# Two recurrent mixers with other engines for their gate products and another order in their last tiles; a gated mixer whose out-projection starts with other banks

## The reference

```python
def _rglru_mixer(h, w_in, conv_w, conv_b, gate_a_w, gate_a_b, gate_x_w, gate_x_b, lam, w_out):
    gate, xr = jnp.split(h @ w_in, 2, axis=-1)          # 1280 columns each
    gate = jax.nn.gelu(gate)
    xr = _causal_dwconv(xr, conv_w) + conv_b            # 4 taps
    xh = xr.reshape(b, s, A_HEADS, A_HEAD_DIM)
    r  = sigmoid(einsum(xh, gate_a_w) + gate_a_b)       # 16 heads of 80
    ig = sigmoid(einsum(xh, gate_x_w) + gate_x_b)
    log_a = -8.0 * r * softplus(-lam)
    a = exp(log_a)
    u = sqrt(-expm1(2.0 * log_a)) * (ig * xr)
    hs = scan over time of h[t] = a[t] * h[t-1] + u[t]
    return (hs * gate) @ w_out

def _sgu_mixer(h, w_in, norm_g, w_s, s_bias, w_out):
    u, v = split(gelu(h @ w_in))
    v = _rmsnorm(v, norm_g)
    mixed = (lower-triangular w_s applied over chunks of 128 tokens to v) + s_bias
    return (u * mixed) @ w_out
```

## Time and profile before

| | us |
|---|---|
| median of 3 runs | 2772.72 (2772.41 to 2773.76) |
| the profiled execution, its own time | 2773.85 |
| its span | 2772.0 |
| TensorE busy | 2708.9 (98%) |
| VectorE busy | 1778.0 (64%) |
| ScalarE busy | 1202.8 (43%) |
| GpSimd busy | 202.2 (7%) |
| mean granted TensorE clock | 0.992 of full |

### The profile page before, as it was taken

How to read it: one execution, slowest core, us unless ns; L and a number is a source line. 1 busy time by engine, 2 the same in 40 slices (tenths; PEclk the granted TensorE clock), 3 DMA queues, 4 the chain that set the end, 5 groups by cost and what they waited for, 6 DMA issues and landing times. The chain is left out here.

```text
span 2772.0 us, 46096 instructions
## 1 busy us (share of the span) xinstructions
PE 2708.9 (98%) x17940; PEld 2422.9 (87%) x17940; DVE 1778.0 (64%) x2341; ACT 1202.8 (43%) x1757; POOL 202.2 (7%) x224
## 2 busy tenths in 40 slices
PE   7999999999999999999999999999999999999998
PEld 4888887688888888888879999999999999998998
DVE  4777535767772377742666558874676578668874
ACT  4232223642322233221455456553655446456553
POOL 1000012000000000000210014100300000004000
PEclk9999999999999999999999999999999999999999
DMA  6555532025563245542326643565656565653564
GB/s 255 190 188 191 164 111 78 16 90 187 187 192 104 91 159 182 186 148 98 124 73 214 198 157 111 172 201 192 209 178 201 182 198 182 198 177 109 184 198 136
DMA packets 153642, 444.59 MB, mean 160 GB/s; under 512 B 46512, under 2 KB 47920, under 8 KB 152880
## 3 DMA queue, kind: packets, MB, share of 16 engines
q1 hardware_dynamic: 119248, 431.38, 47.3%
q0 software_dynamic: 1120, 11.27, 1.1%
q10 hardware_dynamic: 33152, 0.26, 0.6%
HBM read 441.68 MB, written 1.18 MB: 160 GB/s over the span
## 5 line engine op out<-in xcount | busy, mean ns | idle before, releaser
L1725 DVE TENSOR_TENSOR wlo<-raw,whi 128x1024 fp32r<-128x1024 f32 x672 | 831.8, 1241 | 572.6 <-ACT whi L1219 569.9
L1219 ACT ACTIVATE whi<-raw 128x1024 fp32r<-128x1024 f32 x672 | 708.2, 1056 | 622.9 <-PE ps L573 575.1
L571 PE MATMUL ps<-nh,whi 128*128 128x512 f32 (+1 forms) x1280 | 498.5, 389 | 3.4 <-DVE nl L1790 1.7
L572 PE MATMUL ps<-nl,whi 128*128 128x512 f32 (+1 forms) x1280 | 492.6, 385 | 0.0
L573 PE MATMUL ps<-nh,wlo 128*128 128x512 f32 (+1 forms) x1280 | 492.4, 385 | 0.0
L571 PE MATMUL ps<-bh,whi 128*128 128x256 f32 x1456 | 404.5, 278 | 0.0
L572 PE MATMUL ps<-bl,whi 128*128 128x256 f32 x1456 | 403.3, 277 | 0.0
L573 PE MATMUL ps<-bh,wlo 128*128 128x256 f32 x1456 | 403.1, 277 | 0.0
L571 PEld LDWEIGHTS ps<-nh,whi 128*128 128x128 f32 x1280 | 241.1, 188 | 73.0 <-issue 12.6
L573 PEld LDWEIGHTS ps<-nh,wlo 128*128 128x128 f32 x1280 | 241.1, 188 | 48.4
L571 PE MATMUL ps<-mh,whi 128*128 (+1 forms) x1024 | 282.7, 276 | 0.0
(11 more groups left out here) (256 smaller groups left out, 4196.6 us busy)
## 6 DMA issues: line engine op xcount, KB each, us to landing
raw<-stream SPq DMA_DIRECT2D x800, 512.0 KB, 3.4
head<-stream SPq DMA_DIRECT2D x8, 1024.0 KB, 14.6
gates_w<-gate_in POOLq DMA_DIRECT2D x2, 3328.0 KB, 13.3
cst<-cst_in POOLq DMA_DIRECT2D x2, 1280.0 KB, 5.8
X<-x_in SPq DMA_DIRECT2D x1, 2048.0 KB, 7.8
out<-X SPq DMA_DIRECT2D x8, 128.0 KB, 2.0
fftw<-fftw_in POOLq DMA_DIRECT2D x2, 256.0 KB, 5.8
sbias<-sb_in POOLq DMA_DIRECT2D x1, 512.0 KB, 4.7
```

The lines of the kernel that those rows point to most:

```text
L571: pe.matmul(dst, w1, rhs_hi, start=start, stop=False)
L572: pe.matmul(dst, w1, rhs_lo, start=False, stop=False)
L1219: act.activation(whi[:, at % RING, :], raw[:, n % RING, :], ACT.Copy).then_inc(w_hi_ready, 1)
L1725: dve.tensor_tensor(wlo[:, r, :], raw[:, PLACE["main", at] % RING, :], whi[:, r, :].bitcast(F32), ALU.subtract).then_inc(w_ready, 1)
```

## The change

It does five things.

1. The two gate products of each tile (`ix = sg * cv`, `ix = ix * dd`) leave GpSimd and become two VectorE instructions at the end of `inverse(m)`.
2. ScalarE takes the first five square roots inside the loop, at m = 7 (`roots(0)`: load of the root table, one instruction over five tiles), and loads the sigmoid table again after it. The other five stay behind the loop. GpSimd multiplies each half into `ix` once its roots are there, on a semaphore of its own (`ix_rooted`).
3. `product(0)` stands on VectorE before the split of slot 19; `product(1)`, `product(2)`, `product(3)` follow the evacuations of tiles 16, 17, 18. Before, `product(0)` to `product(3)` followed those of tiles 16 to 19.
4. ScalarE does `b_upper(0)` before it loads the gelu table, and `b_upper(1)`, `b_upper(2)`, `b_upper(3)` after the gelus of tiles 15, 16, 17. Before, `b_upper(0)` to `b_upper(3)` followed those of tiles 16 to 19.
5. The gated mixer's out-projection no longer waits at its start. Its first slot takes the banks in the order 4, 5, 0, 1, 2, 3, 6, 7, and waits before bank 0 for the evacuations, before bank 6 for `gated(6)` and before bank 7 for `gated(7)`.

```diff
--- before.py
+++ after.py
@@ -72,7 +72,9 @@
 
 HEAD_G = 4
 
-RNN_TAIL = [(), (), (0,), (1,), (2,), (3,)]
+RNN_EARLY = 4
+RNN_TAIL = [(), (1,), (2,), (3,), (), ()]
+ROOTS_AT = 7
 
 
 SGU_TURN = [(), (0, 1), (2, 3), (4,), (5,), (6,), (7,), ()]
@@ -436,6 +438,7 @@
         dd_ready = sem("dd_ready")
         av_ready = sem("av_ready")
         ix_ready = sem("ix_ready")
+        ix_rooted = sem("ix_rooted")
         gate_mm = sem("gate_mm")
         root_ready = sem("root_ready")
         small_loaded = sem("small_loaded")
@@ -511,7 +514,8 @@
             return AT[f"in{l}"] + i
 
 
-        FREE_ORDER = {0: [4, 5, 6, 7, 0, 1, 2, 3], 3: [6, 7, 0, 1, 2, 3, 4, 5]}
+        FREE_ORDER = {(0,): [4, 5, 6, 7, 0, 1, 2, 3], (3,): [6, 7, 0, 1, 2, 3, 4, 5],
+                      (0, 6, 7): [4, 5, 0, 1, 2, 3, 6, 7]}
 
         OUT_K = [4, 5, 6, 7, 0, 1, 2, 3]
 
@@ -833,9 +837,10 @@
                 for n, k in enumerate(order[:-2]):
                     weights(at + n)
                     pe.wait_ge(*readies[n])
-                    for m in (FREE_ORDER[free[2]] if n == 0 and free else range(KD)):
-                        if n == 0 and free and m == free[2]:
-                            pe.wait_ge(*free[:2])
+                    for m in (FREE_ORDER[tuple(f[0] for f in free)] if n == 0 and free else range(KD)):
+                        for bank_, freed, count in (free or () if n == 0 else ()):
+                            if m == bank_:
+                                pe.wait_ge(freed, count)
                         ins = mm3(bank(m, w), at + n, m, src_h[:, k, 0:w], src_l[:, k, 0:w], n == 0, False)
                     ins.then_inc(slots_done, 1)
                 n = len(order) - 2
@@ -1105,7 +1110,7 @@
                 pe.wait_ge(gate_ready, c["cv"])
                 keep_busy(4, 14)
                 short_down(f"b_out{i}", S, oh, ol, range(NR), [(b_lo, c["blo"] + k + 1) for k in range(NR)],
-                           free=(b_evac, c["bev"], 0))
+                           free=[(0, b_evac, c["bev"])])
                 c["blo"] += NR
 
             def sgu(i):
@@ -1168,9 +1173,8 @@
                     for k in SGU_TURN[m]:
                         turn(k)
                 c["bev"] += 2 * KD
-                pe.wait_ge(b_f32, c["blo"] + KD)
                 short_down(f"b_out{i}", S, oh, ol, range(KD), [(b_lo, c["blo"] + k + 1) for k in range(KD)],
-                           free=(b_evac, c["bev"], 0))
+                           free=[(0, b_evac, c["bev"]), (6, b_f32, c["blo"] + KD - 1), (7, b_f32, c["blo"] + KD)])
                 c["blo"] += KD
 
             def conv(i):
@@ -1189,7 +1193,7 @@
                         if m == 0 and q == 2:
                             input_rows(True)
                 short_down(f"b_out{i}", S, oh, ol, range(KD), [(b_lo, c["blo"] + k + 1) for k in range(KD)],
-                           free=(b_f32, c["blo"] + KD, 3))
+                           free=[(3, b_f32, c["blo"] + KD)])
                 c["blo"] += KD
 
             for i, kind in enumerate(MIXERS):
@@ -1561,7 +1565,7 @@
                     act.wait_ge(gate_mm, c["cv"] + m + 1)
                     if m >= 2:
 
-                        act.wait_ge(ix_ready, 3 * c["cv"] + 2 * (m - 2) + 1)
+                        act.wait_ge(ix_ready, 2 * c["cv"] + 2 * (m - 2) + 1)
                         act.wait_ge(th_ready, c["cv"] + m - 1)
                     act.activation(sg[:, m % 2, 0:S], ps[:, 4 + m % 2, 0:S], ACT.Sigmoid,
                                    bias=vcol("ba", j * NR + m))
@@ -1580,6 +1584,13 @@
 
                     act.wait_ge(dd_ready, c["cv"] + m + 1)
                     act.activation(av[:, m, :], dd[:, m % 3, :], ACT.Copy, bias=-1.0, scale=2.0).then_inc(av_ready, 1)
+
+                def roots(h):
+
+                    act.preload_act_table(ACT.Sqrt)
+                    act.wait_ge(minus_ready, c["cv"] + 5 * h + 5)
+                    act.activation(th[:, 5 * h:5 * h + 5, :], th[:, 5 * h:5 * h + 5, :], ACT.Sqrt,
+                                   scale=-4.0).then_inc(root_ready, 1)
 
                 split_to(at + 5)
                 copy_rows(True)
@@ -1598,6 +1609,9 @@
                     if m >= 2:
                         sigmoids(m - 2)
                         one_minus(m - 2)
+                    if m == ROOTS_AT:
+                        roots(0)
+                        act.preload_act_table(ACT.Sigmoid)
                 tail = HEAD_G + NR
                 split_to(at + tail + 3)
                 decayed(NR - 4)
@@ -1608,22 +1622,18 @@
                 one_minus(NR - 1)
                 split_to(at + tail + 5)
 
-                act.preload_act_table(ACT.Sqrt)
-                for h in range(2):
-                    if h:
-                        act.wait_ge(minus_ready, c["cv"] + NR)
-                    act.activation(th[:, 5 * h:5 * h + 5, :], th[:, 5 * h:5 * h + 5, :], ACT.Sqrt,
-                                   scale=-4.0).then_inc(root_ready, 1)
+                roots(1)
                 for m in range(NR - 3, NR):
                     decayed(m)
                 c["cv"] += NR
+                b_upper(oh, 0)
                 act.preload_act_table(ACT.Gelu_apprx_tanh)
                 for n in range(tail, 2 * NR):
                     gate_part(n, 1)
                     for m in RNN_TAIL[n - tail]:
                         b_upper(oh, m)
                 c["bev"] += 2 * NR
-                for m in range(RNN_TAIL[-1][-1] + 1, NR):
+                for m in range(RNN_EARLY, NR):
                     split_to(AT[f"b_out{i}"] + m - 1)
                     b_upper(oh, m)
                 c["b"] += NR
@@ -2225,9 +2235,15 @@
                     dve.wait_ge(minus_ready, c["cv"] + m + 1)
                     if m >= 3:
 
-                        dve.wait_ge(ix_ready, 3 * c["cv"] + 2 * (m - 2))
+                        dve.wait_ge(ix_ready, 2 * c["cv"] + 2 * (m - 2))
                         dve.wait_ge(av_ready, c["cv"] + m - 2)
                     dve.reciprocal(dd[:, m % 3, :], av[:, m, :]).then_inc(dd_ready, 1)
+
+                    dve.wait_ge(gate_ready, c["cv"] + m + 1)
+                    dve.tensor_tensor(ix[:, m, :], sg[:, m % 2, S:T], cv[:, m, :], ALU.mult).then_inc(ix_ready, 1)
+                    dve.wait_ge(ix_ready, 2 * c["cv"] + 2 * m + 1)
+                    dve.wait_ge(dd_ready, c["cv"] + m + 1)
+                    dve.tensor_tensor(ix[:, m, :], ix[:, m, :], dd[:, m % 3, :], ALU.mult).then_inc(ix_ready, 1)
 
                 def tap(m, t):
 
@@ -2254,7 +2270,7 @@
 
                 def product(m):
 
-                    dve.wait_ge(ix_ready, 3 * c["cv"] + 2 * NR + m + 1)
+                    dve.wait_ge(ix_rooted, c["cv"] + m + 1)
                     dve.wait_ge(av_ready, c["cv"] + m + 1)
                     link(dve.tensor_tensor_scan(hs[:, m % 2, :], av[:, m, :], ix[:, m, :], 0.0, ALU.mult, ALU.add))
                     if m >= 2:
@@ -2270,13 +2286,14 @@
                 gate_part(tail + 1)
                 inverse(NR - 2)
                 inverse(NR - 1)
+                product(0)
                 split_to(at + tail + 5)
                 for n in range(tail + 2, 2 * NR):
                     evac(gelu_g[:, n - NR, :], n, at)
-                    for m in RNN_TAIL[n - tail]:
-                        product(m)
+                    if n - tail - 1 < RNN_EARLY:
+                        product(n - tail - 1)
                     split_to(at + n + 4)
-                for m in range(RNN_TAIL[-1][-1] + 1, NR):
+                for m in range(RNN_EARLY, NR):
                     product(m)
                     split_to(AT[f"b_out{i}"] + m - 1)
                 b_lower(oh, ol, NR - 1)
@@ -2468,21 +2485,11 @@
                     pool.memset(xpad[:, :, 0:3], 0.0).then_inc(pads_ready, 1)
                     for m in range(NR):
 
-                        pool.wait_ge(gate_ready, c["cv"] + m + 1)
-                        pool.wait_ge(cv_ready, c["cv"] + m + 1)
-                        pool.tensor_tensor(ix[:, m, :], sg[:, m % 2, S:T], cv[:, m, :], ALU.mult
-                                           ).then_inc(ix_ready, 1)
-                        pool.wait_ge(ix_ready, 3 * c["cv"] + 2 * m + 1)
-                        pool.wait_ge(dd_ready, c["cv"] + m + 1)
-                        pool.tensor_tensor(ix[:, m, :], ix[:, m, :], dd[:, m % 3, :], ALU.mult
-                                           ).then_inc(ix_ready, 1)
-                    for m in range(NR):
-
                         if m % 5 == 0:
                             c["root_b"] += 1
                             pool.wait_ge(root_ready, c["root_b"])
-                            pool.wait_ge(ix_ready, 3 * c["cv"] + 2 * NR)
-                        pool.tensor_tensor(ix[:, m, :], ix[:, m, :], th[:, m, :], ALU.mult).then_inc(ix_ready, 1)
+                        pool.wait_ge(ix_ready, 2 * c["cv"] + 2 * m + 2)
+                        pool.tensor_tensor(ix[:, m, :], ix[:, m, :], th[:, m, :], ALU.mult).then_inc(ix_rooted, 1)
```

## The result

The changed kernel takes 2782.60 us (median of 7 runs, 2780.40 to 2782.86), the kernel before 2773.65 beside it (7 runs, 2770.59 to 2775.52): ratio 1.0029, 95% interval 1.0019 to 1.0038. The profiled execution took 2782.86, its span is 2780.7.

A forecast was written before the change was run, and what follows sets the result against it. TensorE, busy 2708.9 of 2772.0 us, bounds the kernel, so only its waits matter. Recurrent mixers +4.1 and +4.2, clock +1.4, gated mixer -3.7 sum to +6.0 us: median 2778.7, range 2769.5 to 2782.

The forecast's parts named there:

- The loop on VectorE: Recurrent loop: two gate products add 0.79 us, period becomes 5.34 instead of 5.54 us per tile.
- Roots inside the loop: ScalarE at m = 7: root block 3.9 us, VectorE stands 2.25 us, GpSimd contention 0.8, gates(7) delayed 1.85 us.
- The drain: Rival at the loop's table loads: 1.38 us extra per switch, 5.5 us more for both mixers, 2784.2; chance 0.03.
- The tail: VectorE after cv tile 8: product(0) at 1725.6 instead of 1724.80; five GpSimd root products cost 1.4 us.
- The handover: Recurrent tail: ScalarE and VectorE alternate on splits and b_upper, 4.04 us per tile instead of 2.86.
- Tile 19: Last gate tile before the recurrent out-projection: evacuated at 1741.4, TensorE resuming 4.1 us later in layer 0, 4.2 in layer 3.
- Clock: TensorE at half speed behind recurrent out-projection waits: no change in layer 0, +1.4 us (0 to 1.6) in layer 3.
- Gated mixer: Its out-projection: wait falls to 0.3 us and the half clock behind it goes, -3.7 us, or -2.4 if clock falls.
- the roots hide: Rival in the loop: ScalarE's 3.9 us fit into its idle time, time 2770.7; chance 0.12.
- the handover does not bind: Rival in the tail: ScalarE's splits come free, VectorE keeps 2.86 us per tile, time 2769.8; chance 0.08.
- GpSimd's ten root products: Rival in the recurrent mixers: each takes 0.5 us of VectorE, 1.8 us more per mixer, 2782.3; chance 0.06.

The follow-up runs named there:

- the filler: Changed kernel plus 11 filler matmuls before TensorE waits for cv tile 8 in gates(7): 2780.60 us, ratio 1.0026 to the kernel before.
- products alone: Kernel before with only its two gate products per tile moved from GpSimd to VectorE: 2774.56 us, ratio 0.9999 to the kernel before.
- both edits: Changed kernel with the first five roots after the loop again and b_upper(1) to (3) one tile later: 2773.74 us, ratio 0.9993 to the kernel before.
- roots behind the loop: Changed kernel with the first five roots after the loop again, on one table load: 2782.45 us, ratio 1.0027 to the kernel before.
- the 12 us: Kernel before with tiles 17 to 19 evacuated earlier, per-bank waits, new gated bank order, gate products on VectorE: 2760.91 us, ratio 0.9954 to before.
- the products one tile later: Changed kernel with ScalarE's b_upper(1), (2), (3) one tile later: 2776.63 us, ratio 1.0000 to the kernel before.
- the gated edit alone: Kernel before with only the gated mixer's out-projection bank order and waits changed: 2772.30 us, ratio 0.9990 to the kernel before.

## Why the prediction was right, and where it was short

The median was forecast at 2778.7 and came at 2782.6: slower as forecast and by the mechanism forecast. It is 0.6 above the upper end of the range as a bare time, but 0.9 of it is the kernel before, which measured 2773.65 this time: as a difference, +6.0 was forecast, the range reached to +9.3, and +8.95 came by the medians, +8.0 by the ratio. By its steps:

- **The loop on VectorE.** Period 5.31 to 5.35, products 0.40 and 0.34 between starts. Right.
- **Roots inside the loop.** Block 3.88 (1699.13 to 1703.01), wait 2.35 against 2.25, split and taps stretched by 0.8 (1.58 and 1.98 against 1.22 and 1.52), gates(7) at 1707.65. Right. The drain that the Trainium skill gives (page "ScalarE: Activation LUTs", section "What ACT_TABLE_LOAD costs") would, as I read it, have put the next instruction 2.66 behind the load; it starts 1.30 behind it, as before.
- **The tail.** `product(0)` came at 1726.66, not 1725.6. This is the step that failed: I took gates(7) as delayed but otherwise unchanged, at full clock. Behind the wait of 2.73 us that the delay itself makes on TensorE, the clock fell; windows of the kernel after (length, PE, PEld, DVE, ACT, POOL, clock, DMA):

```profile
1708.00:1709.00 1.00, 1.00 (x6) 0.90 (x5) 1.00 (x1) 0.00 (x0) 0.00 (x0) 0.93 0.45 180
...
1711.00:1712.00 1.00, 1.00 (x4) 0.82 (x3) 0.96 (x3) 0.27 (x1) 0.00 (x0) 0.50 0.00 0
```

  TensorE's lateness reached ScalarE's sigmoids, the split of slot 18 behind them, and with a wait of 1.22 VectorE. With the filler `product(0)` starts 81.27 behind the mixer's start, where 81.4 was forecast; without it at 82.51. At tile 19 the filler took 0.86 away.
- **The handover.** 4.05 us per tile against 4.04. Right; undone, it is 2.86.
- **Tile 19.** 97.96 behind the mixer's start, forecast 97.2, and 97.10 with the filler: the missing term is the whole difference. A path of kernels gives the sum of +4.86: gate products -0.87 (before to products alone), the new places of `product(0)` to `product(3)` and of `b_upper(0)` +1.67 (to both edits), handover +2.76 (to roots behind the loop), root block +1.30 (to after). Of the +1.67, 1.39 is plain work: before the change three products stood ahead of tile 19's evacuation, after it all four do, and one takes VectorE 1.39 (2.86 less a split of 1.14 and an evacuation of 0.33). The path makes the split between the last three: with the roots taken early, `product(0)` finds them ready, and part of the +1.67 would not be there without the other edits.
- **Clock.** After the 5.1 us waits TensorE stays at half speed until about 1746.4 and 2569.0, 1.8 us lost for each against 1.4 forecast; layer 0 had lost 1.6 already. The term was a little too small, and "7 instead of 12 per us" was a poor measure: these counts take in every record that reaches into the window. By the distance of starts, 0.213 us at half clock against 0.113, a microsecond of half clock costs 0.47. In a second profile of the kernel after layer 3 lost only 1.6. Layer 3's +7.49 is 4.96 for the resumption, 1.8 for the clock and 0.7 for the pitch of its matmuls.
- **Gated mixer.** -3.63 against -3.7, 0.24 us of wait left against 0.3, first matmul 0.39 us and so at full clock. Right.

In sum, layer 0 was forecast at +4.1 and took +5.0, layer 3 at +5.6 and took +7.5, the gated mixer was met. The 0.7 of the pitch is luck of that execution and no part of the change.

The rivals: that the roots hide is refuted by the wait of 2.35, though the kernel that undoes the block is no faster beyond noise; that the handover does not bind is refuted by the waits of 1.10 and by the kernel that undoes it, 8 us faster. That GpSimd's ten root products take 1.8 us more of VectorE per mixer than forecast is refuted too: two met the loop (0.8 us, as forecast), and with the filler tile 19 comes at 97.10, where 97.2 was forecast with 1.4 us for the five of the tail.

## What to carry to other kernels

When an edit makes the busiest engine wait at a new place, price that wait's effect on the clock and follow it once round the loop: here tile 19 came 0.86 us later than the wait's own length explained. When two engines share a queue of splits, look whether the work of one tile sits in front of the other's split and behind its own; here that cost 2.4 to 2.8 us at the last tile, and about 2 more in clock behind the longer wait. And what frees the resource that the bound engine wants (here a bank) goes ahead of what it does not need yet: with a wait for each bank that brought some 8 of the 12 us, with no less work, and the gated mixer's banks 3.7.

## What the runs showed of the hardware

TensorE's matmuls of 128x256 come at one of two pitches at a granted clock of 1.00, 0.1133 or 0.1178 us, and a whole out-projection keeps one of them. Windows of ten microseconds in the out-projections of layers 0 and 3, of the kernel after in its first profile and in a second:

```profile
1749.00:1759.00 10.00, 10.00 (x91) 10.00 (x89) 8.99 (x14) 5.29 (x8) 0.00 (x0) 1.00 0.59 196
2572.00:2582.00 10.00, 10.00 (x88) 10.00 (x87) 8.77 (x13) 4.88 (x8) 0.00 (x0) 1.00 0.55 187
```

```profile
1748.00:1758.00 10.00, 10.00 (x87) 10.00 (x87) 8.93 (x14) 4.73 (x8) 0.00 (x0) 1.00 0.54 195
2570.00:2580.00 10.00, 10.00 (x90) 10.00 (x90) 9.02 (x15) 5.32 (x8) 0.00 (x0) 1.00 0.59 204
```

> The kernel after once more, for one profile. Open: in its first profile the matmuls of layer 3's out-projection stood 0.1178 us apart at a granted clock of 1.00, those of layer 0's 0.1133 us apart (0.0045 x some 150 matmuls at full clock = 0.7 us). Theory: the two pitches come and go between executions, whatever the kernel does; then the pitches of the three out-projections (layers 0, 1, 3) come out otherwise than 0.1133, 0.1134, 0.1178 in this profile, while the waits stay at 5.1 and 5.1 us and the two waits in the loop at 2.7. Rival: the change makes layer 3 slow, and its pitch is 0.1178 again with the other two at 0.1133.

> The kernel before once more, for one profile, for the same question. In its first profile all three out-projections had 0.1133 us per matmul. Theory: at least one of the three is 0.1178 here, or they are the same by chance (about one in three or four stages has been slow so far). Also whether the clock falls behind the wait of 2.6 us in layer 0 and not in layer 3 again: if it falls at random, the terms for the clock of the two layers are each worth a half.

The second profile of the kernel after (2780.41 us) has the slow pitch in layer 0 and not in layer 3, with the same waits (5.1 and 2.7): the pitch belongs to the execution, not to the kernel. In the second profile of the kernel before all three were 0.1133 again, which at the rate seen elsewhere may be chance. Over the 14 profiles, 14 of 42 out-projections were slow, each by 4%, about 1 us. What decides it stays open. Stages that no edit touched vary as well: in the profile with the products one tile later the feed-forwards behind layers 1 and 2 took 179.9 and 179.8 us, in all others 176.5 to 176.7. So one profile's difference of a few microseconds is read by stages, not by its total.

The clock is as fickle behind a short wait. After 2.6 us at the out-projections it was 0.50 in layer 0 of both profiles of the kernel before and in layer 3 of the second (2560 to 2561), but not in layer 3 of the first. With the gated edit alone it stayed at 1.00 in layer 0 (1737 to 1738) and was 0.50 in layer 3, and with the products one tile later it fell in neither: four of eight such waits. After the 1.9 us for slot 19, with the roots behind the loop, it was 0.50 in layer 0 of both kernels and stayed at 1.00 in layer 3 of both. Windows of layer 3 with the gated edit alone, and of layer 0 with the roots behind the loop:

```profile
2554.00:2555.00 1.00, 1.00 (x6) 1.00 (x6) 1.00 (x2) 0.42 (x1) 0.00 (x0) 0.50 0.86 332
```

```profile
1727.00:1728.00 1.00, 1.00 (x7) 1.00 (x6) 1.00 (x2) 0.67 (x2) 1.00 (x3) 0.50 0.90 344
```

After the 2.73 us in the loop the gate matmuls took 4.23 to 4.54 us in each of the six rows read. So a term for the clock behind such a wait is worth a chance, not a fixed price.
